# A two-block transformer kernel on one Trainium2 core: the later layers' Fourier part rewritten and placed inside v's unit

## The reference

```python
u = rmsnorm(x, norm1_g[l]) @ w_in[l]          # q, k, v, glu_in, four_in
att = diff_attention(q, k, v, lam)            # 8 heads, two components each
y_a = rmsnorm(att, subln_g[l]) * (1 - lam_init) @ w_proj_a[l]
y_b = silu(layernorm(conv31(ga * sigmoid(gb)) + conv_b)) @ w_proj_b[l]
fc = four_in.reshape(b, s, 4, 128)            # s = 256 tokens
fr = fft.fft2(fc, axes=(1, 3), norm='ortho').real
y_c = fr.reshape(b, s, 512) @ w_proj_c[l]
gates = sigmoid(h @ w_gate[l] + b_gate[l])    # 3 branches of 1024
x = x + (gates[0]*y_a + gates[1]*y_b + gates[2]*y_c) @ w_out[l]
x = x + (silu(f_gate) * f_up) @ w_ffn_out[l]
```

## Time and profile before

| | |
|---|---|
| three executions | 1243.1, 1242.74, 1243.14 us |
| the profiled execution's own time | 1242.84 us |
| its span, from first to last instruction | 1241.5 us |
| TensorE (PE) busy | 1236.1 us, 6638 matmuls |
| VectorE (DVE) busy | 954.6 us, 1389 instructions |
| ScalarE (ACT) busy | 722.9 us, 1024 instructions |
| GpSimd (POOL) busy | 439.3 us |
| DMA | 233.74 MB, mean 188 GB/s |

### The profile page before, as it was taken

One profiled execution on the slowest core, in us unless ns is written; L12 is line 12 of the kernel. 1 busy time (PEld: TensorE's weight loads), 2 busy tenths in 40 slices (PEclk: granted clock), 3 DMA queues, 4 the chain that ended last, 5 costly groups with the idle time before them and its releaser, 6 DMA issues.

```text
span 1241.5 us, 17116 instructions
## 1 busy us (share of the span) xinstructions
PE 1236.1 (100%) x6638; PEld 1055.3 (85%) x6638; DVE 954.6 (77%) x1389; ACT 722.9 (58%) x1024; POOL 439.3 (35%) x354
## 2 busy tenths in 40 slices
PE   9999999999999999999999999999999999999999
PEld 8987788888888889888888888888988888888887
DVE  6865667677787478985878888976898587888895
ACT  7755545377775365577836555546457674655552
POOL 0011231039882079377420112008747750012100
PEclk9999999999999999999999999999999999999999
DMA  9753335555555448644554554465865454555442
GB/s 360 274 197 136 136 119 172 194 187 178 203 176 197 169 170 278 204 160 174 177 211 170 189 184 166 173 223 185 285 181 197 148 175 164 204 183 191 160 164 117
DMA packets 39007, 233.74 MB, mean 188 GB/s; under 512 B 4752, under 2 KB 5392, under 8 KB 13072
## 3 DMA queue, kind: packets, MB, share of 16 engines
q1 hardware_dynamic: 38928, 232.67, 53.5%
HBM read 225.31 MB, written 1.05 MB: 182 GB/s over the span
## 4 chain that ended last, share of the span: by engine, by line
PE 98%; DVE 1%; DMA 0%; ACT 0%; SPq 0%; issue 0%
PE ps L656 19%; PE ps L563 18%; PE ps L565 18%; PE ps L564 18%; PE ps L661 10%; PE ps L568 5%; PE ps L582 2%; PE ps L624 1%; PE ps L623 1%; PE ps L622 1%; PE ps L724 1%; PE ps L1212 1%; DMA raw<-in_w 0%; PE ps L894 0%; PE ps L809 0%; PE ps L810 0%
## 5 line engine op out<-in xcount | busy, mean ns | idle before, releaser
L1302 ACT ACTIVATE whi<-raw 128x2048 fp32r<-128x2048 f32 (+1 forms) x212 | 400.2, 1891 | 117.2 <-PE ps L565 105.2
L2074 DVE TENSOR_TENSOR wlo<-raw,whi 128x2048 fp32r<-128x2048 f32 x168 | 388.2, 2316 | 89.4 <-ACT whi L1302 88.4
L1900 POOL TENSOR_TENSOR wlo<-raw,whi 128x512 fp32r<-128x512 f32 x176 | 229.1, 1336 | 88.5 <-ACT whi L1302 85.5
L656 PE MATMUL ps<-hh,whi 128*128 128x512 f32 x1056 | 255.9, 392 | 0.9 <-DVE x L2522 0.9
L656 PEld LDWEIGHTS ps<-hh,whi 128*128 128x128 f32 x1056 | 192.9, 188 | 37.7 <-ACT whi L1302 1.3
L563 PE MATMUL ps<-whi,hh 128*128 128x512 f32 (+1 forms) x504 | 200.8, 398 | 0.0
L565 PE MATMUL ps<-whi,hh 128*128 128x512 f32 (+1 forms) x504 | 195.4, 388 | 0.0
L564 PE MATMUL ps<-wlo,hh 128*128 128x512 f32 (+1 forms) x504 | 195.1, 387 | 0.0
L1872 POOL TENSOR_TENSOR st<-st,sm 128x1 f32<-128x1 f32 (+2 forms) x28 | 45.1, 1609 | 309.5 <-DVE st L2128 229.3
L661 PEld LDWEIGHTS ps<-hh,wlo 128*128 128x128 f32 x1056 | 137.8, 191 | 6.7
L661 PE MATMUL ps<-hh,wlo 128*128 128x256 f32 x1056 | 139.8, 282 | 0.0
(11 more groups left out here) (347 smaller groups left out, 2063.7 us busy)
## 6 DMA issues: line engine op xcount, KB each, us to landing
raw<-in_w SPq DMA_DIRECT2D x202, 1024.0 KB, 4.9
raw<-in_w SPq DMA_DIRECT2D x12, 256.0 KB, 6.4
gain<-in_bias SPq DMA_DIRECT2D x12, 256.0 KB, 5.1
kst<-kh SPq DMA_DIRECT2D x16, 128.0 KB, 2.9
qst<-qh SPq DMA_DIRECT2D x16, 128.0 KB, 2.3
raw<-in_w SPq DMA_DIRECT2D x2, 560.0 KB, 11.2
x<-in_x SPq DMA_DIRECT2D x4, 256.0 KB, 6.2
gain<-in_rows SPq DMA_DIRECT2D x2, 512.0 KB, 5.7
```

Source lines behind the costliest of these rows:

```text
L656: pe.op.matmul(o[:, :], wh[:, k, c], t.hh[:, k, :, :], start=k == 0, stop=False, skip_group_check=True)
L1302: act.op.activation(t.whi[i % NHI][:, c], t.raw[i % NRAW][:, c], ACT.Copy).then_inc(*at("act_hi", ("hi", i)))
L1900: pool.op.tensor_tensor(t.wlo[i % NRAW][:, half(k)], t.raw[i % NRAW][:, half(k)], t.whi[i % NHI][:, half(k)].bitcast(F32), ALU.subtract).t ...
L2074: dve.op.tensor_tensor(t.wlo[i % NRAW][:, c], t.raw[i % NRAW][:, c], t.whi[i % NHI][:, c].bitcast(F32), ALU.subtract).then_inc(*at("dve_lo ...
```

## The change

Fourier part. The transform over 256 tokens is split by the symmetry of its matrices: token n and token n + 128 have the same cosine and sine at even frequencies and opposite ones at odd frequencies. So DVE folds the two halves of the input: from xf0 (copied by ACT as before) and the bank of half 1 it writes their difference to xf[1] and their sum to xf[0] (halves_folded). TensorE multiplies xf[0] with the even frequencies of csT and xf[1] with the odd ones, one product of 128 columns each. ACT puts the frequencies back in order as it copies to T12. Over channels, cosines (129 columns) and sines (127) are now two separate products; ACT copies the sines to a tile (sines_out), and DVE forms cosines less sines and, mirrored, cosines plus sines (mirrored) into t.fr. ACT then takes the upper part from t.fr and DVE the lower.

Place. The part is no longer a stage between v and attention, but three bursts in v's unit, behind its steps 3, 5 and 7. Seeds 3 to 5 are issued behind v's unit. In the taps of the convolution, 10 of the 20 of the Fourier stage go to attention.

Start. The first quarter of x is issued by ACT as its first instruction, not by SP, and the zero products are 22 and 17 where they were 28 and 34.

The diff, cut to its core:

```diff
+BEFORE, BETWEEN = 3, (2, 2, 1)
-    t.csT = at("csT", y + 14, [128, 2, S])
-    t.cdT = at("cdT", y + 18, [128, 3, 128])
+    t.csT = at("csT", y + 14, [128, 2, 128])
+    t.cdT = at("cdT", y + 18, [128, 2, 128])
+    t.fr = [at(f"fr{i}", y + 11 + 2 * i, [128, S]) for i in range(2)]
+    t.sines = [at(f"sines{i}", y + (15, 15.5625)[i], [128, 129]) for i in range(2)]
...
     load("d_small", t.sm[:, 0:NEARLY], d["in_small"][:, 0:NEARLY], ("small",))
-    load_x(0, 0)
...
-    warm(28)
+    warm(22)
     pe.wait_ge(*on("small"))
     first_turned(0, 0)
-    warm(34)
+    warm(17)
...
-        run(rows(f"v{l}", *h))
+        def over_tokens(g):
+            for tt in range(2):
+                pe.wait_ge(*on("free", (f"xf{l}", tt)))
+            pe.wait_ge(*on("cs", l))
+            pe.wait_ge(*on("T12", l, g - 2) if g >= 2 else on("free", ("q", l, "T", g)))
+            for odd in range(2):
+                product(t.sc[g % 2][:, odd * 128:odd * 128 + 128], t.xf[odd][:, g * 128:g * 128 + 128],
+                        t.csT[:, odd, :], names=[("fourier 1", l, g)] * odd)
+        def over_channels(k):
+            pe.wait_ge(*on("T12", l, k))
+            pe.wait_ge(*on("cd", l))
+            pe.wait_ge(*on("fr sums", l, k - 2) if k >= 2 else on("free", ("k", l, "T", 1 - k)))
+            o, T = (t.ob, t.tp)[k % 2], t.T12[k % 2]
+            product(o[:, 0:129], t.cdT[:, 0, :], T[:, 0:129])
+            product(o[:, 129:256], t.cdT[:, 1, :], T[:, 129:256], names=[("fourier 2", l, k)])
         def fourier():
-            for g in range(5):
...
+            for g in (0, 1):
+                over_tokens(g)
+            yield BETWEEN[0]
+            for k in (0, 1):
+                over_channels(k)
+            for g in (2, 3):
+                over_tokens(g)
+            yield BETWEEN[1]
+            for k in (2, 3):
+                over_channels(k)
+            yield BETWEEN[2]
+        g = rows(f"v{l}", *h)
+        steps(g, BEFORE)
+        weave(fourier(), g)
+        run(g)
...
-        weave(chain(fourier(), attention(), after_attention()), back, 2)
+        weave(chain(attention(), after_attention()), back, 2)
...
+    act.op.dma_start(t.x[:, 0, half(0)], d["in_x"][tok(0), half(0)]).then_inc(*at("d_x0", ("x", "in", 0, 0), by=16))
...
+        def tokens_out(g):
+            act.wait_ge(*on("fourier 1", l, g))
+            if g >= 2:
+                act.wait_ge(*on("fourier 2", l, g - 2))
+            act.op.activation(t.T12[g % 2][:, :].rearrange("p (m o) -> p m o", o=2),
+                              t.sc[g % 2][:, 0:S].rearrange("p (o m) -> p m o", o=2), ACT.Copy).then_inc(
+                *at("act_out", ("T12", l, g)))
+        def sines_out(k):
+            act.wait_ge(*on("fourier 2", l, k))
+            act.wait_ge(*(on("fr sums", l, k - 2) if k >= 2 else on("sines ends", l)))
+            act.op.activation(t.sines[k % 2][:, 1:128], (t.ob, t.tp)[k % 2][:, 129:256], ACT.Copy).then_inc(
+                *at("act_small", ("sines", l, k)))
...
+            for k in (2, 3):
+                sines_out(k)
+            for k in (2, 3):
+                upper(("fr hi", l, k), t.frh[:, k, :], t.fr[k - 2][:, :], ("fr sums", l, k))
+            yield BETWEEN[2]
+        g = rows(f"v{l}", value_out(f"v{l}", lambda tt: t.v2[tt][:, :], []))
+        steps(g, BEFORE)
+        weave(fourier(), g)
+        run(g)
+        if l == 0:
+            act.wait_ge(*on("x", "f3", 1, 1))
+        for k in (3, 4, 5):
+            seed(k)
...
+        def halves_folded(tt):
+            if tt == 0:
+                return
+            name = (f"xf{l}", 1)
+            dve.wait_ge(*on("free", (f"xf{l}", 0)))
+            dve.wait_ge(*on("got", *name))
+            dve.op.tensor_tensor(t.xf[1][:, :], t.xf[0][:, :], bank(name)[:, :], ALU.subtract).then_inc(*at("dve_out"))
+            await_own("dve_out")
+            dve.op.tensor_tensor(t.xf[0][:, :], t.xf[0][:, :], bank(name)[:, :], ALU.add).then_inc(
+                *at("dve_out", ("free", name)))
...
+        def mirrored(k):
+            o, f = (t.ob, t.tp)[k % 2], t.fr[k % 2]
+            dve.wait_ge(*on("sines", l, k))
+            dve.op.tensor_tensor(f[:, 0:129], o[:, 0:129], t.sines[k % 2][:, :], ALU.subtract).then_inc(*at("dve_out"))
+            dve.op.tensor_tensor(f[:, 129:256], o[:, 127:0:-1], t.sines[k % 2][:, 127:0:-1], ALU.add).then_inc(
+                *at("dve_out", ("fr sums", l, k)))
...
         def fourier():
+            for i in range(2):
+                dve.op.memset(t.sines[i][:, 0:129:128], 0.0).then_inc(*at("dve_out", *([("sines ends", l)] * i)))
+            yield BETWEEN[0]
+            for p in range(2):
+                for k in (2 * p, 2 * p + 1):
+                    mirrored(k)
+                conv_some(3)
+                for k in (2 * p, 2 * p + 1):
+                    fourier_lower(k)
+                yield BETWEEN[p + 1]
...
+        conv_some(4)
```

More of the change, by code:

```diff
@@ L1177, in layer @@
         qk_turned("q")
-        run(rows(f"v{l}", *h))
-        def fourier():
-            for g in range(5):
[L1182 to L1200, removed]
@@ L1209, in attention @@
                     if tt == 0:
-                        pe.wait_ge(*on("WT", l, hd - 1) if hd else on("fr", l, 3))
+                        pe.wait_ge(*on("WT", l, hd - 1) if hd else on("fr sums", l, 3))
                     for k in range(2):
@@ L1738, in layer @@
                 qk_upper("k")
-        run(rows(f"xf{l}", copied_rows(f"xf{l}", lambda tt: t.xf[tt][:, :])))
+        first = copied_rows(f"xf{l}", lambda tt: t.xf[0][:, :])
+        run(rows(f"xf{l}", lambda tt: None if tt else first(0)))
         qk_upper("q")
-        run(rows(f"v{l}", value_out(f"v{l}", lambda tt: t.v2[tt][:, :], [])))
-        if l == 0:
-            act.wait_ge(*on("x", "f3", 1, 1))
         done = []
@@ L1780, in gate_out @@
             return out
[L1783 to L1795 removed]
+        def tokens_out(g):
[10 more added lines that the diff above has]
+                *at("act_small", ("sines", l, k)))
+        def fourier():
+            for g in (0, 1):
+                tokens_out(g)
+            yield BETWEEN[0]
+            for k in (0, 1):
+                sines_out(k)
+            for g in (2, 3):
+                tokens_out(g)
+            for k in (0, 1):
+                upper(("fr hi", l, k), t.frh[:, k, :], t.fr[k][:, :], ("fr sums", l, k))
+            yield BETWEEN[1]
+            for k in (2, 3):
+                sines_out(k)
+            for k in (2, 3):
[9 more added lines that the diff above has]
+            seed(k)
         lw = st[:, 128:160].rearrange("p (h t c) -> p h t c", h=8, t=2)
@@ L2751, in layer @@
                 conv_some(4)
-        for _ in rows(f"xf{l}"):
+        def halves_folded(tt):
[8 more added lines that the diff above has]
+                *at("dve_out", ("free", name)))
@@ L2753, in layer @@
+        for _ in rows(f"xf{l}", halves_folded):
             conv_some(2)
         qk_lower("q")
-        for _ in rows(f"v{l}", value_out(f"v{l}", t.v2[0][:, :], [])):
-            conv_some(2)
-        def fourier():
-            for g in range(5):
-                if g >= 1:
-                    k = g - 1
-                    lower([("fr", l, k)], t.frl[:, k, :], (t.ob, t.tp)[k % 2][:, 0:256], t.frh[:, k, :], ("fr hi", l, k))
-                conv_some(3 if g else 8)
-                yield 0
+        def mirrored(k):
[4 more added lines that the diff above has]
+                *at("dve_out", ("fr sums", l, k)))
@@ L2766, in layer, with v_rows @@
+        def v_rows():
+            for _ in rows(f"v{l}", value_out(f"v{l}", t.v2[0][:, :], [])):
+                conv_some(2)
+                yield
+        g = v_rows()
+        steps(g, BEFORE)
+        weave(fourier(), g)
+        run(g)
+        conv_some(4)
         lw = st[:, 128:160].rearrange("p (h t c) -> p h t c", h=8, t=2)
```

26 lines of the change are left out of this document (9 added, 17 removed).

## The result

**The kernel became slower by 0.2%: 1245.46 us (median of 19 runs, 1243.46 to 1247.02) against 1242.69 (19 runs, 1241.95 to 1244.02); ratio 1.0021, 95% interval 1.0014 to 1.0027.** The forecast was 1239.1, with a range of 1237.3 to 1241.4. The runs before lie within 2.1 us; after, they lie in three clusters, near 1243.6, 1245.4 and 1246.7, with a mean granted clock of 0.999, 0.997 and 0.996, where every run of the kernel before that has a clock on record shows 1.000. The profiled execution is the fastest, 1243.46 us (span 1242.2).

The account below looks back on a forecast made before the run. TensorE, busy for the whole span, was taken to bound the kernel. 1242.84 less 6.56 (products) plus 3.0 (waits) less 0.4 (start) gave 1238.9, with 0.26 added back 1239.1 us; range 1237.3 to 1241.4.

Parts of the forecast that it names:

- Part 1, the products: Fourier products on TensorE: fewer and narrower records save 3.28 us a layer, 6.56 for both.
- Part 2, the timetable: Layout of v's unit on TensorE, DVE and ACT: no burst waits, v's last step ends at 515.58.
- two lowers (0.66): DVE between the frequency sums: forming two lower parts of fr takes 0.66 us.
- Part 3, the wait: TensorE between v and the first gate unit: waits for ACT's copy and seed, 1.5 us a layer, 3.0 both.
- DVE is late: Rival, 17%: slow or reversed reads on DVE lengthen the wait behind v to 1.9 to 2.4 a layer, 1239.9 to 1240.9.
- TensorE falls to 1.2 GHz after the new gap: Rival, 3%: first gate unit of each layer runs at low clock, 2.75 us a layer, 1244.6.
- Part 4, attention: Ten taps a layer move into attention, 3.9 us of DVE; it reaches the first maximum in time, nothing paid.
- Part 5, the start: Kernel start: x issued by ACT lets the weight quarters go out earlier, 0.4 us saved, bounds 0 and 0.6.
- the third rival: 10%: the start gives nothing, or the clock rises later there, 0.4 to 1.0 us lost, 1239.5 to 1240.1.

Follow-up runs that it names:

- e2: Changed kernel with POOL's split of the second gate's first chunk held until DVE has written the lower parts of fr 0 and 1; 1239.35 us.
- e8: Changed kernel with the three Fourier bursts one step of v earlier (2 steps ahead, then 2, 2 and 2); 1241.00 us.
- e5: Changed kernel with the old start: x's first quarter issued by SP, 28 and 34 zero products; 1245.08 us.
- e3: Changed kernel with eleven added fp32 products of 128 columns, never read, in TensorE's wait behind v; 1242.27 us.
- e1: Changed kernel with the first seed behind v issued by ACT before the third burst instead; 1239.07 us.
- e6: Changed kernel with both the first seed issued before the third burst and POOL's split held behind the lower parts of fr 0 and 1; 1238.22 us.
- e4: Kernel before with the start edits alone: x's first quarter issued by ACT, 22 and 17 zero products; 1242.90 us.

## Why the prediction was wrong, point by point

- **Part 1, the products: right.** The point at which v and the Fourier part are both done came at 515.30 (forecast 515.58, before 518.86). Less 0.18 for the start that is 3.4 us in layer 0 against 3.28. The gate units of the two layers start 398.46 us apart before (518.77, 917.23) and 398.10 after, of which 2.94 are the new gap, so layer 1 saves 3.3: 6.7 for both.
- **Part 2, the timetable: right in all but one term, and this is the step that failed.** Steps, bursts, taps and sums came within 0.3 us (its terms from 509.82 add up to 514.62, where it has 514.55). The wrong term is "two lowers (0.66)". It was taken from a row of an instruction with one input in PSUM, for one with both in SBUF, and beside it no account was taken of what POOL does at that time. It measured 2.15. The change's own text shows the swap of operand (the lower part is now formed from fr), and the trace of before had both POOL's split at that time and, at 602.28, what such a collision costs. e2 takes the collision away, and the term is 0.67 again (511.26 to 511.93).
- **Part 3, the wait: mechanism right, size wrong by that term.** The forecast's law, each 0.1 us of DVE's lateness adds 0.1, held: DVE's next sums are 1.25 us late (515.80 for 514.55) and v's end is 0.28 early, and 1.42 with both added is 2.95, measured 2.94. That is 1.4 above the 1.5 taken. Where DVE is in time (e2) the wait is what was forecast. For two layers the difference is 2.9 us.
- **The rival "DVE is late" (17%)** had the right direction, but its bounds (1.9 to 2.4 a layer, from the pace of reads) left out 2.94, since pace was not the cause.
- **The rival "TensorE falls to 1.2 GHz after the new gap" (3%)** is what carried the kernel to slower. Its place was right, its price (2.75 a layer) lies near the long fall (2.7) and above the short one (1.6). Its chance was wrong because it was weighed for a gap of 1.5 us alone; in e2 and e8, with 1.3 us idle, the clock indeed never fell in 19 runs, and with 2.78 it fell at least once in each of the 30 runs of the changed kernel and e5. The two rivals were treated as separate, when the first is the condition of the second. The late DVE without a fall is what e3 shows: 1242.27, above the 1239.9 to 1240.9 given for it. Whether the clock falls after gaps between 1.3 and 2.78 us no run shows.
- **Part 4, attention: right for the change, wrong as a reason.** DVE was not waited for after v, because TensorE itself came 2.8 us late. As soon as TensorE is in time (e1, e6), DVE takes the first maximum over 2 us after the scores, and 1 us a layer is lost.
- **Part 5, the start: wrong, at its lower bound.** 0.4 was taken, nothing that can be measured came (e4). TensorE went on at 9.61 for 9.79, and the same start varies by more than that. The later rise of the clock that the third rival feared cost e4's runs nothing either. By the rule of the Trainium skill cited there, "DMA: Bandwidth & Descriptors", on issuing engines not being separate DMA queues, the term is 0; the runs agree.

The sum with the measured terms, against the profiled execution: 1238.9 forecast, 0.2 more for the start, 0.1 less for the products, 2.9 for the two waits and 1.6 for one short fall give 1243.5; it took 1243.46. The median run, 1245.46 with a clock of 0.997, must have a longer fall, or a second one; it has no trace.

What stays open is why a gap of the same length is followed by a long fall, a short one or none: layer 0 of the changed kernel's trace has a gap of 2.78 us and no fall, that of e5 one of 2.77 and a long one.

## What to carry to other kernels

When a change swaps an operand from PSUM to SBUF, its old duration is no longer evidence: look at what POOL runs at that time, and put the two apart in time if it collides. Look too for the same collision elsewhere in the trace of before: it may already be priced there. A gap of 2.8 us in TensorE had a second price here, in its clock, which one of 1.3 us had not; so two rivals of which one brings about the other get one joint case. Filling the gap with products that nobody reads is a cheap test (and gave 3.2 us back). And when an engine is freed, price the others as if it came in time: what was covered by its own lateness is the next wait.

## What the runs showed of the hardware

- DVE forming the lower part from two SBUF tiles of 256 columns: 0.41 us alone (0.75 for two), 0.80 and 1.50 us beside POOL's split of four pieces, which itself took 5.39 instead of 5.03 us. Of the eight groups of two in layer 0 (changed kernel, e1, e2, e8) the four beside POOL took 2.23, 2.23, 1.65 and 2.32 us, the others 0.74 to 0.76. DVE with one input in PSUM was not held up (q's lower parts 1.28 us for two with and without POOL, taps 0.39), nor was ACT (two upper parts read from fr in SBUF took 0.72 us beside POOL, from 510.77, and 0.81 without it, from 516.31). POOL's pieces take 1.28 us, and an instruction held until a piece ends loses up to that: the excess is 0.4 and 1.1 us here, and 1.1 us for DVE's chunk of 2048 columns in the trace of before (3.40 for 2.3; POOL's next piece took 3.37), 0.3 where only 0.4 us of the piece was left (2.56). The Trainium skill, "SBUF — State Buffer", on who interferes with whom, states that a DVE instruction with two SBUF inputs contends with a GpSimd instruction that reads SBUF, and that the contention is an exclusive lock. The runs agree with the first; the sizes fit the second.
- The granted clock: amid full work, after 2.78 us of idle TensorE, it fell to 0.5 (1.2 GHz), from the first product on in two cases (916.34, and e5 at 517.93) and a microsecond after the restart in a third (e5: restart 918.77, products 0.23 apart until 919.76); after the fourth such gap (518.24) it did not fall. A fall cost 1.6 or 2.7 us. With 1.3 us idle (e2, e8) none of 19 runs fell, and with the 2.78 us filled by added products to 0.33 (e3) none of 11.
